# A hybrid mixer and mixture-of-experts layer: tile 7's router, the counts and the gates in another order between the row projection and the routed loop

## What is computed

```python
x <- LayerNorm(ALPHA * x + TokenMixer(x))
x <- LayerNorm(ALPHA * x + MoE(x))

scores = sigmoid(xt @ router_w.T)                      # 64 experts, 8 groups
biased = scores + router_b
...                                                    # best 4 groups, then best 6 experts
gate = gate / sum(gate) * ROUTE_SCALE
...                                                    # tokens sorted by expert, in blocks of 128 rows
y_rows = (silu(h @ wg[e]) * (h @ wu[e])) @ wd[e]       # for each block
routed = segment_sum(y_rows * row_gate)
shared = (silu(xt @ sh_wg) * (xt @ sh_wu)) @ sh_wd
return routed + shared
```

## Time and profile before

| | |
|---|---|
| timed runs, median (lowest to highest) | 2021.8 us (2021.01 to 2022.92) |
| the profiled execution, its span | 2028.3 us |
| TensorE matmul busy | 1958.8 us, 97% |
| VectorE, ScalarE, GpSimd busy | 66%, 46%, 30% |
| HBM traffic over the span | 210 GB/s |

### The profile page before, as it was taken

How to read it: one execution, slowest core, us unless ns; L and a number is a source line. 1 busy time by engine, 2 the same in 40 slices (tenths; PEclk the granted TensorE clock), 3 DMA queues, 4 the chain that set the end, 5 groups by cost and what they waited for, 6 DMA issues and landing times. The chain is left out here.

```text
span 2028.3 us, 32259 instructions
## 1 busy us (share of the span) xinstructions
PE 1958.8 (97%) x9395; PEld 1476.0 (73%) x9396; DVE 1339.6 (66%) x2553; ACT 926.5 (46%) x1605; POOL 617.3 (30%) x411
## 2 busy tenths in 40 slices
PE   8999999999999999989999989999999999999995
PEld 7887787877768766657868647777777777677772
DVE  2794643444106677779767748787777787788866
ACT  2111221244212244451034247777777777677762
POOL 2443232323322211002143633333333333233332
PEclk9999999999999999999999999999999999999998
DMA  6122322122522210046770577999999999999969
GB/s 203 42 73 89 120 64 72 46 83 63 139 88 83 73 61 25 22 162 231 241 282 32 198 260 239 308 377 345 330 343 320 359 329 328 333 327 327 333 167 241
DMA packets 171618, 393.28 MB, mean 194 GB/s; under 512 B 28016, under 2 KB 101009, under 8 KB 146832
## 3 DMA queue, kind: packets, MB, share of 16 engines
q1 hardware_dynamic: 131600, 301.13, 41.1%
q0 software_dynamic: 30720, 74.28, 14.9%
q10 hardware_dynamic: 9216, 16.78, 2.2%
HBM read 341.20 MB, written 84.46 MB: 210 GB/s over the span
## 5 line engine op out<-in xcount | busy, mean ns | idle before, releaser
L648 PE MATMUL a_bank<-x_hi,w_hi 128*128 128x512 f32 x928 | 373.3, 402 | 0.0
L648 PE MATMUL a_bank<-x_hi,w_lo 128*128 128x512 f32 x928 | 362.6, 391 | 0.0
L648 PE MATMUL a_bank<-x_lo,w_hi 128*128 128x512 f32 x928 | 361.7, 390 | 0.0
L2256 DVE TENSOR_TENSOR u_lo<-w_gu,u_hi 128x1024 fp32r<-128x1024 f32 x225 | 268.2, 1219 | 37.0 <-ACT u_hi L1928 29.3
L1928 ACT ACTIVATE u_hi<-w_gu 128x1024 fp32r x225 | 230.6, 1066 | 19.3 <-SPq L1456 18.8
L2271 DVE TENSOR_TENSOR d_lo<-w_d,d_hi 128x1024 fp32r<-128x1024 f32 x152 | 179.5, 1222 | 87.3 <-ACT d_hi L2036 86.3
L583 POOL CAST w_hi<-w_raw 128x1024 fp32r<-128x1024 f32 x56 | 64.8, 1158 | 560.9 <-PE a_bank L648 539.7
L1745 PE MATMUL e_bank<-u_hi,x_g_hi 128*128 128x512 f32 x450 | 207.5, 461 | 0.0
L648 PEld LDWEIGHTS a_bank<-x_hi,w_hi 128*128 128x128 f32 x928 | 174.5, 188 | 40.7 <-issue 6.1
L648 PEld LDWEIGHTS a_bank<-x_hi,w_lo 128*128 128x128 f32 x928 | 174.3, 188 | 37.9
L648 PEld LDWEIGHTS a_bank<-x_lo,w_hi 128*128 128x128 f32 x928 | 174.9, 188 | 33.9 <-issue 0.5
(11 more groups left out here) (376 smaller groups left out, 3594.0 us busy)
## 6 DMA issues: line engine op xcount, KB each, us to landing
w_gu<-in_moe_wg SPq DMA_DIRECT2D x64, 1024.0 KB
w_gu<-in_moe_wu SPq DMA_DIRECT2D x64, 1024.0 KB
w_d<-in_moe_wd SPq DMA_DIRECT2D x64, 1024.0 KB
w_raw<-in_w_in SPq DMA_DIRECT2D x53, 512.0 KB, 3.9
gates<-gate_out ACTq DMA_DIRECT2D x64, 256.0 KB, 2.0
g_sb<-gates SPq DMA_DIRECT2D x16, 1024.0 KB, 5.5
acc_odd<-zero POOLq DMA_DIRECT2D x9, 512.0 KB, 14.6
work<-in_w_out SPq DMA_DIRECT2D x4, 1024.0 KB, 8.9
```

The source lines that it names most:

```text
L648: ins = pe.matmul(bank[h][:, :], w[:, c % 2, k, :], x[:, k, cols], start=(k == 0 and j == 0), stop=(k == KD - 1 and j == 2))
L2256: dve.tensor_tensor(up_part(u_lo[j]), up_weights(slot, j), up_part(u_hi[j]).bitcast(F32), ALU.subtract).then_inc(u_lo_dve, 1)
```

## The change

The order of the calls is changed on three engines; the number of products, transposes, gates and transfers stays.

- `shared_up` takes a range of k steps instead of a half, so that other work can stand at any step.
- TensorE: `router(6)` comes ahead of `counts(4)` and of the shared products; `counts(5)` stands between k steps 1 and 2 of `shared_up(0)`; `turn_x1(7)` between k steps 5 and 6 of `shared_up(1)`; `counts(6)` ahead of `router(7)`; `counts(7)` right behind `shared_turn(0)`; `blocks()` ahead of the second half of `shared_up(3)`; the register reads ahead of `shared_down(2)`; `shared_up(4)` is cut into k 0 to 1 (ahead of `shared_down(3)`), k 2 to 5, and k 6 to 7 behind `turn(0)`.
- VectorE: `chosen(5)`, `put(4)` and `put(5)` come ahead of `normed1(7)`; `shared_hidden(2)` comes behind the block table, `shared_sum(0)` behind the words.
- ScalarE: the sigmoids of tiles 5 and 6 come ahead of the last square root, `shared_gated(0)` ahead of the copy of tile 7, `shared_gated(1)` behind the last sigmoid, and the others follow two tiles ahead.

```diff
--- before.py
+++ after.py
@@ -1689,14 +1689,14 @@
                     if part == 0 and t == NT - 1:
                         ins.then_inc(wo_hi_read, 1)
                 ins.then_inc(mix_done, 1)
-            def shared_up(t, part=None):
+            def shared_up(t, ks=range(KD)):
                 s = t % 2
-                if t >= 2 and part != 1:
+                if t >= 2 and 0 in ks:
                     pe.wait_ge(s_silu, t - 1)
-                for k in range(KD) if part is None else range(4 * part, 4 * part + 4):
+                for k in ks:
                     ins = pe.matmul(bank[s][:, :], turned_x1(t)[:, k, :], (s_gu if t <= NU else tail_gu)[:, k, :], start=k == 0,
                                     stop=k == KD - 1)
-                if part != 0:
+                if KD - 1 in ks:
                     ins.then_inc(s_gu_done, 1)
 
             def shared_turn(t):
@@ -1838,36 +1838,39 @@
                 if t:
                     router(t - 1)
                 turn_x1(t)
+            router(NT - 2)
             counts(NT - 4)
             pe.wait_ge(e_in, EARLY_LOADS)
             pe.wait_ge(s_gu_in, 32)
             pe.wait_ge(pre_read, NT - 1)
-            shared_up(0)
-            router(NT - 2)
+            shared_up(0, range(2))
+            counts(NT - 3)
+            shared_up(0, range(2, KD))
+            shared_up(1, range(6))
             turn_x1(NT - 1)
-            shared_up(1, 0)
-            counts(NT - 3)
+            shared_up(1, range(6, KD))
+            counts(NT - 2)
             router(NT - 1)
-            shared_up(1, 1)
-            counts(NT - 2)
-            shared_up(2, 0)
+            shared_up(2)
             shared_turn(0)
-            shared_up(2, 1)
+            counts(NT - 1)
+            shared_up(3, range(4))
             shared_down(0)
-            counts(NT - 1)
             shared_turn(1)
-            shared_up(3)
+            blocks()
+            shared_up(3, range(4, KD))
             shared_down(1)
             shared_turn(2)
-            blocks()
-            shared_down(2)
             n = trips(pe)
             e_first = expert_of(pe, 0)
+            shared_down(2)
             shared_turn(3)
+            shared_up(NU, range(2))
             shared_down(3)
+            shared_up(NU, range(2, 6))
             pe.wait_ge(s_ht_out, NU)
-            shared_up(NU)
             turn(0, 0, 16)
+            shared_up(NU, range(6, KD))
             pe.wait_ge(s_silu, NU + 1)
             for part in range(2):
                 up(0, 0, e_first, part)
@@ -1975,18 +1978,19 @@
                 act.activation(x1_n[:, t, :], x1_n[:, t, :], ACT.Copy, scale=ALPHA).then_inc(xa_ready, 1)
                 if t:
                     x1_turned(t - 1)
-                if 2 <= t < NT - 1:
+                if t >= 2:
                     scored_rows(t - 2)
+                if t == NT - 1:
+                    scored_rows(NT - 2)
                 act.wait_ge(mv_done, t + 1)
                 act.activation(sd[:, t % 2:t % 2 + 1], mv[:, t % 2, 1:2], ACT.Sqrt, bias=eps[:, 0:1]).then_inc(sd_done, 1)
                 if t + 2 < NT:
                     merged_high(t + 2)
-            scored_rows(NT - 3)
-            scored_rows(NT - 2)
+            act.wait_ge(x1_done, NT)
+            shared_gated(0)
             x1_turned(NT - 1)
             scored_rows(NT - 1)
-            act.wait_ge(x1_done, NT)
-            shared_gated(0)
+            shared_gated(1)
             act.wait_ge(x1_stored, 16 * NT)
             for t in range(NU):
                 s = t % 2
@@ -1995,8 +1999,8 @@
                     act.wait_ge(s_down, t - 1)
                 act.activation(hid_t[t % 2], bank[4][:, 0:2 * P].rearrange('p (j c) -> p j c', j=2), ACT.Copy
                                ).then_inc(s_ht_out, 1)
-                if t + 1 < NU:
-                    shared_gated(t + 1)
+                if t + 2 < NU:
+                    shared_gated(t + 2)
                 for i in range(NU, NT) if t == 0 else ():
                     act.activation(x1_n[:, i, :], x1_n[:, i, :], ACT.Copy, scale=ALPHA).then_inc(x_scaled, 1)
                 if t >= 2:
@@ -2175,7 +2179,7 @@
                     dve.tensor_tensor(wo_lo[:, 4 * part + k, :], w_out[:, 4 * part + k, :], wo_hi[part][:, k, :].bitcast(F32),
                                       ALU.subtract).then_inc(wo_lo_ready, 1)
             dve.wait_ge(ln_in, 32)
-            for t in range(NT):
+            for t in range(NT - 1):
                 normed1(t)
                 if t == 1:
                     dve.wait_ge(e_in, EARLY_LOADS)
@@ -2195,15 +2199,16 @@
                 s = t % 2
                 dve.wait_ge(s_y, t + 1)
                 dve.tensor_tensor(s_acc[:, s, :], s_acc[:, s, :], s_row[:, s, :], ALU.add).then_inc(s_acc_ready, 1)
+            chosen(NT - 3)
+            put(NT - 4)
+            put(NT - 3)
+            normed1(NT - 1)
             chosen(NT - 2)
-            put(NT - 3)
             shared_hidden(0)
+            put(NT - 2)
             chosen(NT - 1)
-            put(NT - 2)
             shared_hidden(1)
             put(NT - 1)
-            shared_hidden(2)
-            shared_sum(0)
 
             c8 = steps
             X(dve.tensor_copy(le[:, :], bank[5][:, 0:E]))
@@ -2222,6 +2227,7 @@
             X(dve.tensor_scalar(ek[:, 2:3], ek[:, 3:4], 8.0, const('even'), ALU.is_lt, ALU.mult))
             X(dve.tensor_scalar(ek[:, 0:1], ek[:, 0:1], float(E - 1), None, ALU.min))
             dve.scalar_tensor_tensor(ek[:, 1:2], ek[:, 1:2], float(E), ek[:, 0:1], ALU.mult, ALU.add).then_inc(ek_done, 1)
+            shared_hidden(2)
             dve.wait_ge(tab_done, 1)
             dve.tensor_copy(table[:, :], bank[5][0:1, 0:2 * MAXB + 1]).then_inc(tab_ready, 1)
             n = trips(dve)
@@ -2295,6 +2301,7 @@
             L = MAXB - 2
             dve.scalar_tensor_tensor(words[:, :], table_f[:, MAXB + 2:2 * MAXB], 1024.0, table_f[:, MAXB:MAXB + L], ALU.mult,
                                      ALU.add).then_inc(words_ready, 1)
+            shared_sum(0)
             shared_hidden(3)
             shared_sum(1)
             dve.wait_ge(words_ready, 1)
```

## The result

The changed kernel takes 2030.64 us, the median of five runs (2029.43 to 2032.38), the kernel before 2022.92 us over five (2021.01 to 2023.43): ratio 1.0046, interval 1.0036 to 1.0057. I had said 2020.5 us, within 2017.5 to 2026.0. The profiled execution of the changed kernel is one of the timed ones: span 2028.8 us, time 2030.64 us, so 1.84 us lie around the span. By the same 1.84 us the profiled execution of before (span 2028.3) took 2030.1 us. None of its timed runs of 2021 to 2023 us is of that length. The two profiles have the same span, although the kernels differ by 7.7 us. That is the first thing to see, and most of the miss lies in it.

The account below looks back on a forecast made before the run. TensorE's queue was taken to bound the stretch before the routed loop, the gather late by only 1.15 us. up(0) at 1204.3 instead of 1205.82 us; 2021.8 less 1.3 gave 2020.5 us, range 2017.5 to 2026.0.

Parts of the forecast that it names:

- The baseline: TensorE before the shared products: weights land at 1141.6 us regardless; 64.15 us from 1141.67 us to up(0), 59.1 of it work.
- The router "costs nothing": router(6) fits the hole before the shared weights land, taking 1.73 us out of TensorE's full stretch.
- the same 1.7 us: Price of the router(6) move if the shared weights land sooner and no longer cover it.
- The cold start of the tail: From turn(0) to up(0): 1.16 + 1.7 + 2.4 us, with no cold clock counted.
- The tail as a gain: Last two k steps of shared_up(4) behind turn(0): 1.7 us of product beside the hand-over, wait before up(0) 2.4 instead of 1.58 us.
- The slots: Slots asked for at 1181.4 us, read 6.5 us behind load_up(3), gather 9.46 us, ending at 1199.0 us.
- The gates: VectorE's chosen(5), put(4), put(5) ahead of tile 7's norm, ending about 1154.9 us; put(7) starts at 1168.7 instead of 1175.68 us.
- `counts(5)` was seen at once: Between k steps of shared_up(0): done at 1145.7 us, just when VectorE needs it; seen 4.8 us late would cost +3.0 us.
- a shift ahead of it passes through to the end: Routed loop from up(0): keeps its old length, so its end moves by as much as its start.
- The table loads: ScalarE: three more table loads at 1.28 us each; only two meet a waiting engine.
- Late results: Rival, 0.22: TensorE's small results are seen late, counts(5) by 4.8 us: +3.0 us, 2024.8 us; with counts(7) late too, 2026.6 us.

Follow-up runs that it names:

- the added wait: Kernel before plus a TensorE wait, behind tile 5's transposes, for ScalarE's copy of them: ratio 1.0000 (0.9989 to 1.0011), 2022.5 us.
- before, copy: Kernel before, unedited, profiled and timed again beside its own runs: ratio 1.0008 (0.9997 to 1.0019), profile span 2028.2 us.
- before, six steps behind the turn, same chip: Kernel before with the last six k steps of shared_up(4) moved behind turn(0): ratio 1.0046, 2032.2 against 2022.45 us.
- changed, copy: Changed kernel, unedited, timed again beside the kernel before: ratio 1.0028, 2036.1 against 2030.95 us; on another chip 1.0018.
- changed, old tail, `blocks` back: Changed kernel with turn(0) again behind all of shared_up(4) and blocks() again behind shared_turn(2): ratio 1.0036 (1.0022 to 1.0049), 2029.9 us.
- the version with the old tail: Changed kernel with only turn(0) put back behind the whole of shared_up(4): ratio 1.0018 (1.0005 to 1.0031), 2033.7 us.

## Why the prediction failed, step by step

The profiles can be put on one scale: us from the start of `router(5)`. No version moves it but the one with the added wait, where TensorE stands 1.17 us ahead of the last row projection.

| | first shared product | `turn(0)` | `up(0)` | loop |
|---|---|---|---|---|
| before, profile on record | 8.60 | 70.01 | 72.75 | 80.92 |
| before, copy | 5.72 | 69.98 | 72.52 | 80.69 |
| before with the wait, at 2022 us | 3.99 | 62.28 | 64.92 | 73.10 |
| before, six steps behind the turn, same chip | 4.21 | 62.23 | 72.75 | 82.62 |
| changed | 9.87 | 67.51 | 72.56 | 82.43 |
| changed, copy | 10.55 | 69.49 | 76.04 | 85.91 |
| changed, old tail, `blocks` back | 9.86 | 70.34 | 72.88 | 81.05 |

**The baseline (the step that failed).** I read a hole ahead of 1141.67 us, wrote "The shared weights land at 1141.6 us whatever I do" and built the sum on a 64.15 us stretch from there. That hole was no property of the kernel. It came from a late-seen result, in an execution that took 2030.1 us. I had the warning in the sum itself: I carried a difference over to a median 6.5 us away without asking where the 6.5 us (with what lies around the span, 8) were. The late row of `counts(3)` stood in my own rival. Against the execution of 2022 us the loop starts 9.3 us later: `turn(0)` 5.2, from there to `up(0)` 2.4, and the cold `up(0)` 1.7. Less 0.8 us for a `router(5)` that starts sooner, that is 8.5 of the 8.9 us between the spans. Against the late one of the record it is 1.5 us later. Late weights are not all that such an execution has: in the copy of before the products start at 5.72 us, only 1.7 us later than at 2022 us, and `turn(0)` is 7.7 us later. There the end of `shared_down(1)` and of `blocks` is seen 4.7 and 4.1 us late (last section), and `shared_down(2)` waits 5.47 us instead of 0.77 and runs 1.5 us longer, cold.

**The router "costs nothing".** It was right for the late case only, and I had named the price if the cover goes: "it costs back the same 1.7 us". That price was too small. With the weights there, the product starts 5.9 us later (9.87 less 3.99), of which 1.7 are the router's own and had to be paid later anyway, so some 4.1 us are lost: the 2.80 us wait for ScalarE, and the half clock that makes the router 1.8 us and `counts(4)` 0.3 us longer, less the 0.8 us for which TensorE stood there before; the first quarter of the product is cold too, 1.3 us more. These 5.4 us are all of the 5.2 that `turn(0)` is later, since the two steps that now stand behind the turn (1.7 us) are made up for by the 1.70 us that it waits for the gather. I had reckoned with the wait for the sigmoid, but beside the weights, and with a router of 1.7 to 1.9 us; it took 3.65. (Not always: in the copy of the changed kernel of the first comparison and in the version with the old tail it took 2.0 us behind the same 2.80 us, and the start of the first product was cold instead.) This is read from profiles. A run that moves the router alone on a chip with prompt results is missing: in mine the results came late. How much would come back is open.

**The cold start of the tail.** From `turn(0)` to `up(0)` it was 5.05 us (said: 5.3), but `up(0)` then took 8.82 us. I had costed no clock there, though I had the cold product of the earlier trace rows in hand. With the old tail none of the nine profiles shows it, with steps behind the turn six of eight.

**The tail as a gain.** The words have "1.7 us of product lie beside the hand-over"; ScalarE needed its 2.0 to 2.2 us after them all the same, as it first gates tile 4, whose product now ends after the turn. The sum was soberer than the words: it adds 1.16, 1.7 and 2.4 us one behind the other. By its own numbers the old tail would have reached `up(0)` at 1198.3 + 1.7 + 1.16 + 1.58 = 1202.7 us, 1.6 us sooner than the 1204.3 us forecast. So the split was a loss on paper already, and I hadn't worked that out. The experiments give 2.4 us of loss for two steps and some 9.8 for six.

**The slots.** Forecast 1181.4 us, measured 1185.61. I had `load_up(3)` only ahead of the read in SyncE's queue; it also holds up the landing of the placements. The read then landed in 4.83 us (said: 6.5) and the gather in 7.39 us from its issue (9.46), so the errors cancel at `turn(0)`: that 1199.0 us was met is luck.

**What held.** The gates fit: `put(7)` starts at 1167.79 us (said: 1168.7). `counts(5)` was seen at once. From its start to the end of the last block the loop is 751.1, 751.2 and 751.8 us long in before, the changed kernel and before with the wait, so a shift ahead of it passes through to the end; over all versions it is 750 to 755 us, a spread of the size of some effects here. The table loads took 1.28 us each, and where ScalarE waited for nothing else the activation followed 1.30 us after the load's start (rows of ScalarE above). The Trainium skill, page "ScalarE: Activation LUTs", section "What ACT_TABLE_LOAD costs", has 2.66 us for a switch; the row has no drain behind the load.

**The rivals.** Late results at 0.22 was the right phenomenon on the wrong side: it sat in the profile that I took as the baseline, and the changed kernel's own was free of it. One reading in that rival was too strong: VectorE was busy until it took `counts(2)` and `counts(6)`, so they don't show when these were seen. Had I asked what the kernel looks like with `counts(3)` seen at once, the weights would have come 5 us sooner, and the router's wait would have stood uncovered.

## What to carry to other kernels

When the profiled execution is some us longer than the timed ones, find the late event in it before any hole near it is used as cover: look for two engines released at the same moment, long after the instruction that both waited for had ended. A step moved behind a wait whose end is set by a transfer is added to the path, even if it looks as if it filled a hand-over. Filling a hole with work that waits for another engine can leave the hole where it is, and the clock can drop with it.

## What was new about the hardware

TensorE's small results were seen late in most executions, though not on every chip. From the end of `counts(3)` to VectorE's next instruction: 4.8 us in the profile of before, 2.0 in its copy (where VectorE was busy until then, and only SyncE's 2.4 us tell), and 4.8 to 8.7 in eleven others (old order and new), but 0.04 us or less in the changed kernel's own profile and in the three of the chip at 2022 us. In six of the thirteen late profiles VectorE and SyncE, which wait for matmuls 0.4 us apart, are released within 0.1 us of each other. In several TensorE's own records show a gap of 0.5 us or more that ends at the moment of the release. The changed kernel with the old tail, TensorE, VectorE and SyncE:

```profile
1123.93 0.39 PE L1776 MATMUL e_bank<-x,e_const 128*128 128x64 f32 x2
...
1131.22 1.64 PE L1788 MATMUL e_bank<-r_t,x_late 128*128 128x64 f32 x13 [0.51 <-issue]
```

```profile
1131.27 0.23 DVE L2160 SCALAR_TENSOR_TENSOR x<-e_bank,e_const 128x64 f32<-128x64 f32 x1 [4.96 <-DMA yt<-reg_b]
```

```profile
1131.20 0.38 SPq L1493 DMA_DIRECT2D sh<-in_sh_wg  x1
```

The matmul has ended, by its record, at 1124.32 us and all three lines say 1131.2 us. It isn't bound to `counts(3)`. In the copy of before `shared_down(1)` ends at 1179.71 us and `blocks` at 1180.48 us, and ScalarE and VectorE, which wait for them, go on within 0.12 us of each other, 4.7 and 4.1 us later; before with the wait has 0.03 and 0.04 us at the same places. TensorE, ScalarE and VectorE of the copy:

```profile
1176.11 3.60 PE L1717 MATMUL e_bank<-sh,work 128*128 128x512 f32 x8
1180.29 0.19 PE L1807 MATMUL e_bank<-e_const,norm 128*1 128x1 f32 x2
1185.95 5.17 PE L1717 MATMUL e_bank<-sh,norm 128*128 128x512 f32 x8 [5.47 <-ACT norm L1996]
```

```profile
1184.44 1.08 ACT L2007 ACTIVATE work<-e_bank 128x512 f32<-128x512 f32 x2 [12.99 <-remote]
```

```profile
1184.56 0.41 DVE L2226 CAST table<-e_bank 1x257 int32<-1x257 f32 x1 [6.13 <-remote]
```

The cause is open. The added wait didn't settle it, as two kernels without it were prompt too on the same chip. That a chip with prompt results runs the kernel before in 2022 us, and the chips with late ones in 2031 to 2035 us, is what the runs show. The spans of the copy of before and of before with the wait differ by 8.3 us, and the two late places of the copy (1.7 us at the start of the products, 6.2 us at `shared_down(2)`) come to 7.9. That the lateness is all of the 8.5 to 12.7 us between the chips is not shown.
